# Values of a hybrid attention layer: projected with weights stationary and turned by transposing DMAs

## The chip, the cores and the metric

The kernel is one program on the 8 cores of a Trainium2 chip. Each core has a TensorE (PE, with its weight loads shown as PEld), a VectorE (DVE), a ScalarE (ACT), a GpSimd (POOL) and a SyncE (SP), and a share of 16 DMA engines. SP and POOL issue nearly all the DMAs. The metric is the device time of the slowest core in microseconds (us). Nothing passes between the cores.

## The reference

Two sequences of 4096 tokens with 2048 channels go through one layer. Cut to what matters:

```
h = rms_norm(x, norm_gain)
q, k, v, z_attn, u_pool, z_pool, gates = split(h @ w_in)     # q, k, v: 3 groups x 8 heads x 128
for g, (window, dilation) in enumerate(((128,1), (512,4), (2048,16))):
    qg, kg = partial_rope(rms_norm(q[g])), partial_rope(rms_norm(k[g]))
    o_g, lse_g = dilated_window_attention(qg, kg, v[g], window, dilation)
attn = softmax over the groups of lse, times o
y_attn = (attn * silu(z_attn)) @ w_branch_attn
y_pool = (multi-scale causal means of u_pool, mapped) * silu(z_pool) @ w_branch_pool
x = x + (sigmoid(gates) . (y_attn, y_pool)) @ w_out
```

Each of the three groups has 8 heads of 128 channels. A query of group g sees the keys t, t-d, t-2d, ... back to t-window.

## The kernel before

**Tiling.** A sequence is cut into four runs of own tokens for four cores; the second sequence does the same on cores 4 to 7. The table KINDS has three kinds of core: kind 0 (cores 0 and 4) has 1168 own tokens and no halo, kind 1 (cores 1 and 5) has 1008 and a halo of 1168, kind 2 (cores 2, 3, 6, 7) has 960 and a halo of 2048. The halo is what group 2, with its window of 2048, needs from before the core's own tokens. Tr and Hr are a sixteenth of the own tokens and of the halo. The program holds three arms and each core runs one; buffers of kind 1 have numbers near 150 to 200 in the profile, those of kind 2 near 240 to 290.

**Stages.** Stage 1 loads x in chunks (halo chunks 0 to 3 in buffers hTh, own chunks 5 and 6 in hX), norms them (squares on ACT, sums at line 756 on DVE for the first two chunks and on POOL for the rest, one matmul at line 760, scaling at line 791 on DVE), and projects keys and values of group 2 for halo and own tokens. They go to the DRAM tensors k2d and v2d. `late_copy` (line 813, on ACT) copies the last 512 halo tokens into hX, strided, since groups 0 and 1 need them. Stage 2 does the three attention groups head by head, stages 3 to 5 the pooling branch, the gates and the output projection.

**Keys and values.** A key projection has a 128 x 128 weight block as the stationary operand and up to 512 tokens moving, 16 matmuls deep (the 2048 channels). Its result has channels on the partitions. It is normed (lines 835 to 847; the sum of squares is a matmul at line 838) and rotated (`rope`, line 860: two small swap DMAs on SP, then three DVE operations). A value projection has it the other way round: tokens are stationary (up to 128 of them, taken with a stride of 1, 4, 8 or 16) and 512 weight columns, four heads, move. So the result has tokens on the partitions, as the product with the attention weights at line 1304 needs them. A tile with fewer than 128 tokens still takes 512 moving columns. Values of groups 0 and 1 are made for four heads at a time (`values`), in buffers vS0 and vS1.

**Order.** A planner (`Flow`) runs every process in an estimated time and writes each engine's instructions down in the order in which they became ready; on the chip each engine runs its list in order and waits on semaphores. It puts a DMA's data at a rate of 0.31 MB per us, and gives each operation a fixed estimate. Weights stream through POOL's queue (line 651, 1 MB of f32 each, cast to bf16) into 16 slots in stage 1 and 8 after it.

Of the kernel before, what the change touches and what calls it, by code (L numbers as in the profile page):

```python
# [400 lines left out]
def build_program():  # L401
    nc = bass.Bass("TRN2", target_bir_lowering=False)
    nwb = sum(4 if k == "v" else 1 for k, _ in weight_order())
# [51 lines left out]
def build_core(nc, sem, ps, io, kind_, Z):  # L455
# [59 lines left out]
    wsl, wq, B_w = [], [], []  # L515
    for hf in range(2):
        wt, _, _ = at(f"w{hf}", OW + 32768 * hf, [128, 8 * KC * 128], BF16)
        wsl += [wt[:, 2048 * i:2048 * i + 2048].rearrange("p (k n) -> p k n", n=128) for i in range(8)]
        wq += [wt[:, 8192 * i:8192 * i + 8192].rearrange("p (k n) -> p k n", n=512) for i in range(2)]
    for i in range(16):  # L520
        B_w.append(S.buf(f"w{i}", OW + 4096 * i, OW + 4096 * (i + 1)))
# [133 lines left out]
    def take(kind, n):  # L655
        k = wtake[0]
        size = 4 if kind == "v" else 1
        wtake[0] += size
        assert (W[k]["kind"], W[k]["n"]) == (kind, n), (W[k], kind, n)
        for j in range(size):  # L660
            yield ("wait", W[k + j]["ev"])
        return got(k, size)

    def got(k, size):
        pos = k if k < NFIRST else (k - NFIRST) % 8
        return dict(t=wq[pos // 4] if size == 4 else wsl[pos], slots=list(range(pos, pos + size)),
                    bufs=[B_w[pos + j] for j in range(size)], need=[W[k + j]["ev"] for j in range(size)])

    def take_later(kind, n):
# [102 lines left out]
    def scales():  # L772
        for c in PREP:
            n = Z.n[c]
            if c < 4:
# [982 lines left out]
```

How the kernel before makes its waits and increments, by code:

```python
        def run(ename, eng):  # L139
            w = {k: 0 for k in sems}
            for o in streams[ename]:
                for k, d in o.deps.items():
                    if d.eng == "pe" and ename == "pe" and not d.isdma:
                        continue
                    if w[k] < d.semval:
                        eng.wait_ge(sems[k], d.semval)
                        w[k] = d.semval
                ins = o.fn(eng)
                if o.signal:
                    ins.then_inc(sems[o.key], 16 if o.isdma else 1)
            for k, v in cnt.items():
                if w[k] < v:
                    eng.wait_ge(sems[k], v)
```

## Time and profile before

| | us |
|---|---|
| median of 3 runs | 1561.34 (1558.42 to 1572.68) |
| profiled execution, whole | 1558.15 |
| its span on the slowest core (core 1) | 1556.5 |
| spans of kind 0, cores 0 and 4 | 1534.1, 1534.8 |
| spans of kind 1, cores 1 and 5 | 1556.5, 1553.3 |
| spans of kind 2, cores 2, 3, 6, 7 | 1551.1, 1546.5, 1546.1, 1551.0 |
| PE busy on core 1 | 1463.6 (94%) |
| ACT, DVE, POOL busy on core 1 | 535.0, 600.0, 158.3 |

PE is named busy from the issue of a matmul to its modelled end, so its share says little on how densely it works. The distance between matmuls of a full stretch does: 512 matmuls of 512 or 496 columns take 108.8 us at the end of the program.

### The profile page before, as it was taken

The numbers are of one execution on the slowest core, as the hardware profiler recorded it, in microseconds if no ns is written. First come the engines' busy times: TensorE is split into PE (matmuls) and PEld (weight loads), VectorE is DVE, ScalarE is ACT, GpSimd is POOL, SyncE is SP. The second block draws the span as 40 slices with busy tenths as digits, with TensorE's granted clock in tenths as the row PEclk, the third lists the DMA queues.
The fourth block names the chain that finished last, engine by engine and source line by source line (L and its number), as shares of the span: only waits on it lengthen the run. The fifth ranks groups of instructions, "written<-read, shape, count | busy, mean of one in ns | idle before, by whom it ended". The sixth has DMA issues, their size and how long they took to land.

```text
span 1556.5 us, 22967 instructions; the slowest of 8 cores (1534.1 to 1556.5 us)
## 1 busy us (share of the span) xinstructions
PE 1463.6 (94%) x7644; PEld 784.6 (50%) x7644; DVE 600.0 (39%) x999; ACT 535.0 (34%) x924; POOL 158.3 (10%) x234
## 2 busy tenths in 40 slices
PE   2579779999999999999999999999999999999997
PEld 1344336659755545555645555544444444444443
DVE  3344166221001667663047767774211222222211
ACT  2554573332113656562155666421111111111000
POOL 1034340010000000000000000000000000000000
PEclk9789889999999999999999999999999999999998
DMA  7964241163524355443254453435444444444973
GB/s 144 172 170 108 83 127 51 44 118 73 112 55 85 68 104 96 70 99 63 43 104 95 75 98 61 85 69 97 78 72 80 78 72 82 80 82 68 226 196 102
DMA packets 98143, 147.19 MB, mean 95 GB/s; under 512 B 50464, under 2 KB 64416, under 8 KB 98016
## 3 DMA queue, kind: packets, MB, share of 16 engines
q0 software_dynamic: 23184, 84.42, 32.1%
q1 hardware_dynamic: 74208, 60.73, 14.0%
q8 instruction: 66, 1.08, 0.3%
q10 hardware_dynamic: 624, 0.46, 0.1%
q14 instruction: 61, 0.50, 0.1%
HBM read 206.95 MB, written 19.01 MB: 145 GB/s over the span
## 4 chain that ended last, share of the span: by engine, by line
PE 89%; DMA 3%; issue 3%; POOL 1%; DVE 1%; ACT 1%; SPq 1%; DVEq 0%; ACTq 0%; POOLq 0%
PE ps L821 68%; PE ps L1622 7%; PE ps L1572 7%; PE ps L838 2%; PE ps L1278 1%; PE ps L1304 1%; POOL s_acc L756 1%; PE ps L1308 1%; DMA s_rota_179<-s_kst_171 1%; PE ps L935 1%; DMA s_xs_159<-xc 1%; DMA s_rota_178<-s_kst_174 1%; DMA s_xs_158<-xc 1%; DMA s_rota_178<-s_kst_171 0%; PE ps L1478 0%
## 5 line engine op out<-in xcount | busy, mean ns | idle before, releaser
L821 PE MATMUL ps<-s_hX,s_w_156 128*128 128x512 bf16 (+3 forms) x3584 | 786.3, 372 | 0.0
L821 PEld LDWEIGHTS ps<-s_hX,s_w_156 128*128 128x128 bf16 x3584 | 351.0, 98 | 375.2 <-issue 4.9
L651 POOL DMA_DIRECT2D s_w_156<-wst x152 | 80.4, 530 | 1149.3 <-PE ps L821 824.5
L821 PE MATMUL ps<-s_w_156,s_hX 128*128 128x512 bf16 (+2 forms) x672 | 147.1, 379 | 0.0
L821 PEld LDWEIGHTS ps<-s_w_156,s_hX 128*128 128x128 bf16 (+2 forms) x672 | 82.5, 123 | 60.8
L1622 PE MATMUL ps<-s_mT,s_w_156 128*128 128x496 bf16 (+1 forms) x512 | 109.0, 376 | 0.0
L1622 PEld LDWEIGHTS ps<-s_mT,s_w_156 128*128 128x128 bf16 x512 | 50.1, 98 | 58.7
L847 DVE SCALAR_TENSOR_TENSOR s_kS_150<-ps,s_cst,s_rr_144 128x384 bf16<-128x384 f32 (+1 forms) x8 | 4.9, 609 | 187.6 <-PE ps L821 182.3
L842 ACT ACTIVATE s_rr_144<-ps 128x512 f32<-128x512 f32 (+3 forms) x72 | 38.0, 528 | 73.8 <-PE ps L838 66.6
L842 ACT ACTIVATE s_rr_145<-ps 128x512 f32<-128x512 f32 (+3 forms) x72 | 38.8, 539 | 61.1 <-PE ps L838 53.7
L1572 PE MATMUL ps<-s_pT,s_w_156 128*128 128x512 bf16 (+1 forms) x256 | 59.6, 376 | 0.0
L1572 PE MATMUL ps<-s_aT,s_w_156 128*128 128x512 bf16 (+1 forms) x256 | 59.6, 376 | 0.0
L821 PE MATMUL ps<-s_w_157,s_hX 128*126 128x512 bf16 x256 | 59.5, 394 | 0.0
L821 PEld LDWEIGHTS ps<-s_w_157,s_hX 128*126 128x126 bf16 x256 | 59.2, 323 | 0.3
L821 PE MATMUL ps<-s_w_157,s_hTh_147 128*73 128x512 bf16 x256 | 59.1, 388 | 0.0
L821 PE MATMUL ps<-s_w_157,s_hTh_148 128*73 128x512 bf16 x256 | 58.8, 391 | 0.0
L835 ACT ACTIVATE s_sq_142<-ps 128x512 bf16<-128x512 f32 (+3 forms) x72 | 38.1, 529 | 37.1 <-PE ps L821 36.0
L835 ACT ACTIVATE s_sq_143<-ps 128x512 bf16<-128x512 f32 (+3 forms) x72 | 38.5, 534 | 32.6 <-PE ps L821 30.0
L760 PE MATMUL ps<-s_acc,s_onesf 128*128 128x292 f32 (+2 forms) x12 | 8.2, 779 | 41.9 <-DVE s_acc L756 34.7
L821 PEld LDWEIGHTS ps<-s_w_157,s_hTh_148 128*73 128x73 bf16 x256 | 30.3, 118 | 27.4 <-issue 3.2
L821 PEld LDWEIGHTS ps<-s_w_157,s_hTh_147 128*73 128x73 bf16 x256 | 30.1, 117 | 27.2 <-issue 3.3
L838 PE MATMUL ps<-s_sq_142,s_ones 128*128 128x512 bf16 (+3 forms) x72 | 25.8, 359 | 18.9 <-ACT s_sq_142 L835 17.1
(308 smaller groups left out, 1532.8 us busy)
## 6 DMA issues: line engine op xcount, KB each, us to landing
s_w_156<-wst POOLq DMA_DIRECT2D x152, 512.0 KB, 5.3
s_w_157<-wst POOLq DMA_DIRECT2D x8, 512.0 KB, 10.3
v2d<-s_vst_175 SPq DMA_DIRECT2D x16, 128.0 KB, 2.1
v2d<-s_vst_176 SPq DMA_DIRECT2D x16, 128.0 KB, 2.0
v2d<-s_vst_177 SPq DMA_DIRECT2D x16, 128.0 KB, 2.1
s_v_199<-v2d SPq DMA_DIRECT2D x4, 512.0 KB, 4.3
s_v_189<-v2d SPq DMA_DIRECT2D x4, 512.0 KB, 4.5
s_xr_215<-xc SPq DMA_DIRECT2D x8, 256.0 KB, 4.0
```

The lines of the kernel that those rows point to most:

```text
L651: yield ("dma", "pool", 1048576, lambda g: g.dma_start(out=wsl[pos][:].rearrange("p k n -> p (k n)"), in_=wst[k]), after, [B_w[pos]], f"w{ ...
L756: yield ("op", eng, dur, lambda v, si=si, n=n: v.tensor_tensor(out=acc[:, 0:n], in0=acc[:, 0:n], in1=sqf[si][:, 0:n], op=ALU.add), [B_acc, ...
L821: yield ("op", "pe", mm_us(n), lambda t, kc=kc, a=lhs(kc), b=rhs(kc): t.matmul(ps[i][0:nr, 0:n], lhsT=a, rhs=b, start=(kc == 0), stop=(kc ...
L835: yield ("op", "act", act_us(n), lambda a: a.activation(out=sq[si][:, 0:n], in_=ps[i][:, 0:n], func=AF.Square), [B_ps[i]], [B_sq[si]])
L838: yield ("op", "pe", mm_us(n), lambda t: t.matmul(ps[ax][:, 0:n], lhsT=ones[:], rhs=sq[si][:, 0:n], start=True, stop=True), [B_sq[si], B_o ...
L842: yield ("op", "act", act_us(n), lambda a: a.activation(out=rr[ri][:, 0:n], in_=ps[ax][:, 0:n], func=AF.Ln, bias=float(128 * EPS)), [B_ps[ ...
L935: yield ("op", "pe", mm_us(n), lambda t, kc=kc, b=mov(kc): t.matmul(ps[i][:, 0:n], lhsT=w["t"][:, kc, :], rhs=b, start=(kc == 0), stop=(kc ...
L1278: yield ("op", "pe", mm_us(n), lambda t, kap=kap, qap=qap, e0=e0, n=n: t.matmul(ps[si][0:rows, e0:e0 + n], lhsT=kap, rhs=qap, start=True, ...
L1304: yield ("op", "pe", mm_us(n), lambda t, vap=vap, nr=nr, e1=e1, cc=cc, n=n, go=go, end=end: t.matmul(nu[:, cc:cc + n], lhsT=vap, rhs=Eb[ei ...
L1308: yield ("op", "pe", mm_us(nd), lambda t, dap=dap, k=k: t.matmul(de[:, c0:c0 + nd], lhsT=ones[0:rows], rhs=dap, start=(k == 0), stop=(k == ...
L1572: b=src[:, h, t0:t0 + n]: t.matmul(ps[yi][:, 0:n], lhsT=a, rhs=b, start=(h == 0), stop=(h == 7)), w["bufs"] + [B_src[h]], [B_ps[yi]])
L1622: b=mT[:, db, t0:t0 + n]: t.matmul(ps[i][:, 0:n], lhsT=a, rhs=b, start=(db == 0), stop=(db == KC - 1)), w["bufs"] + [B_mT[db]], [B_ps[i]])
```

## The change

Values are projected as keys are: a 128 x 128 weight block of one head is stationary and the tokens move. The result has channels on the partitions, and has to be turned. In stage 1 each piece goes to v2d as it is, and the load of a head's v2 tile is a transposing DMA. In stage 2 values of groups 0 and 1 are evacuated by ACT into buffers vt0 and vt1, and a transposing DMA on SP (`turned`) writes the token tiles vS0 and vS1, which are now for one head and double-buffered. The weights of the values come one block for each head. The tokens are split 1184/1024/944/944. The halo of kind 1 has three chunks (444, 370, 370 columns) instead of four of 292. The halo copy is cut into 8 pieces for each chunk and runs on POOL at a lower priority. The load of the masks and the tables and two memsets wait for the last values of stage 1.

```
-KINDS = ((1168, 0), (1008, 1168), (960, 2048))
+KINDS = ((1184, 0), (1024, 1184), (944, 2048))
...
-    o = [("b", BK + 16 + h) for h in range(8)] + [("v", 48 + 16), ("v", 48 + 20)]
+    o = [("b", BK + 16 + h) for h in range(8)] + [("b", BV + 16 + h) for h in range(8)]
+    for h in range(8):
+        o += [("b", BV + h), ("b", BV + 8 + h), ("b", BK + h), ("b", BQ + h), ("b", BK + 8 + h), ("b", BQ + 8 + h),
+              ("b", BQ + 16 + h), ("b", BZA + h)]
...
+        k = -(-16 // (512 // self.Hr)) if H else 0
+        self.halo = list(range(k))
+        cut = [-(-16 * c // k) for c in range(k + 1)] if H else []
+        self.res = {c: (cut[c], cut[c + 1] - cut[c]) for c in self.halo}
...
-        yield ("op", "act", 2.0, lambda a: a.copy(out=dst, in_=src), B_hTh[hi], [B_late[c]])
+        r0, k = Z.res[c]
+        for kc in range(0, KC, 2):
+            yield ("op", "pool", 1.2, lambda g, kc=kc: g.tensor_copy(out=dst[:, kc:kc + 2], in_=src[:, kc:kc + 2]),
+                   B_hTh[hi][kc:kc + 2], [B_late[c]])
...
+    def spill(h, c, src, B, t, sem_, done):
+        k = 128 * (Z.to if c == "own" else Z.res[c][1])
+        yield ("dma", "sp", 131e3, lambda s: s.dma_start(
+            out=v2d[h, :, 128 * t:128 * t + k], in_=src[:, 0:k]), [B], [B_v2d[(h, c)]], sem_)
...
+    def value_piece(c, h, i):
+        yield ("op", "act", act_us(n), lambda a: a.copy(
+            out=vst[vi][:, 0:128 * k].rearrange("p (r l) -> p r l", r=k)[:, :, 0:Hr],
+            in_=ps[i][:, 0:n].rearrange("p (r l) -> p r l", r=k)), [B_ps[i]], [B_vst[vi]])
...
+    def own_piece(vi, m, i, cnt, e):
+        yield ("op", "act", act_us(n), lambda s: s.copy(
+            out=vst[vi][:, 0:128 * k].rearrange("p (r l) -> p r l", r=k)[:, :, l0:l0 + n // k],
+            in_=ps[i][:, 0:n].rearrange("p (l r) -> p r l", r=k)), [B_ps[i]], [B_vst[vi]])
...
+        if H:
+            first += [(c, "v", h) for h in range(NHEAD) for c in (C0, C1)]
...
+        seq = [(5, "k")] + [(c, what) for c in Z.halo[2:] for what in "kv"] + [(6, "k")] if H else []
...
+        for h in range(NHEAD):
+            w = w2[("v", h)]
+            for m, (a, n) in enumerate(own):
+                i = yield from project(P_pp, lambda kc: w["t"][:, kc, :], lambda kc: hX[:, kc, a:a + n], n,
+                                       lambda kc: rd(kc) + w["bufs"])
+                F.spawn(own_piece(vi, m, i, cnt, e), HIGH)
...
-            part(lambda s: s.dma_start(out=v2[i][:, 0:16, :], in_=v2d[h, :, 0:16, :]), hv, B_v2[i], f"lv{i}")
-        part(lambda s: s.dma_start(out=v2[i][:, t0:NV2, :], in_=v2d[h, :, t0:NV2, :]), ov, B_vo[i], f"lw{i}")
+        part(lambda s: s.dma_start_transpose(out=v2[i][:], in_=v2d[h, :, 0:128 * NV2]),
+             [B_v2d[(h, c)] for c in Z.halo + ["own"]], [B_v2[i], B_vo[i]], f"lv{i}")
...
+    def values(g, h, V):
+        w = yield from take("b", BV + 8 * g + h)
+        a0 = LT - (128, 512)[g] * hp
+        for a, n in pieces(a0, NX):
+            i = yield from project(P_pp, lambda kc: w["t"][:, kc, :], lambda kc: hX[:, kc, a:a + n], n,
+                                   lambda kc: rd(kc) + w["bufs"])
+            F.spawn(v_evac(i, dst, n, B_vt, cnt, e), HIGH)
+        F.spawn(turned(g, V, e), MID)
+
+    def turned(g, V, e):
+        vi = yield ("acq", P_vS[g])
+        yield ("wait", e)
+        yield ("dma", "sp", 300e3, lambda s: s.dma_start_transpose(out=vs[vi][:], in_=vt[:]), [B_vt], [B_v[vi]],
+               f"tv{g}{vi}")
...
+        for h in range(NHEAD):
+            V = [{}, {}, None]
+            for g in range(2):
+                yield from values(g, h, V[g])
+            for g in range(3):
+                if g < 2:
+                    yield from keys(g, h, K)
+                yield from queries(g, h, Q)
+                F.spawn(unit(g, h, K, Q, V[g]), MID)
+            yield from gate_z(h)
```

**SP, one head in stage 2, kind 1.** Before, a head's rows on SP are the loads of the keys and values of group 2 for a later head, and the swaps of `rope` (rotb is their target):

```order
L860 DMA s_rotb_204<-s_kS_151 16x1136 x2
L1045 DMA s_k_198<-k2d 128x16x73
L1048 DMA s_k_198<-k2d 128x1008
L1050 DMA s_v_199<-v2d 128x2048
L1055 DMA s_v_199<-v2d 128x1024
L860 DMA s_rotb_203<-s_qT_155 16x1008 x2
L860 DMA s_rotb_204<-s_kS_153 16x1520 x2
```

In the changed kernel a head's rows on SP are these, from its first value tile to its last query:

```order
L1108 DMA_TRANSPOSE s_vS_231<-s_vt_228 128x9x128
L1059 DMA s_k_234<-k2d 128x16x74
L1062 DMA s_k_234<-k2d 128x1024
L1065 DMA_TRANSPOSE s_v_235<-v2d 128x24x128
L1108 DMA_TRANSPOSE s_vS_233<-s_vt_229 128x12x128
L859 DMA s_rotb_240<-s_kS_169 16x1152 x2
L859 DMA s_rotb_239<-s_qT_173 16x1024 x2
L859 DMA s_rotb_240<-s_kS_171 16x1536 x2
L859 DMA s_rotb_239<-s_qS_237 16x1024 x2
L859 DMA s_rotb_240<-s_qS_238 16x1024 x2
```

Three transposing DMAs, of 9, 24 and 12 tiles of 128 x 128, now stand in one row ahead of all five swaps of the head.

**PE, start of stage 2, kind 1.** Before, the values of four heads come first, tokens stationary (a row's first number is how many):

```order
L821 MATMUL ps<-s_w_156,s_hX 128x512 x128
L821 MATMUL ps<-s_w_156,s_hX 112x512 x16
L821 MATMUL ps<-s_w_156,s_hX 128x512 x32
L821 MATMUL ps<-s_w_156,s_hX 124x512 x16
L821 MATMUL ps<-s_w_156,s_hX 128x512 x32
```

In the changed kernel one head's values of groups 0 and 1 come first (weights 174 and 175), then its keys and queries (176, 177):

```order
L820 MATMUL ps<-s_hX,s_w_174 128x384 x48
L820 MATMUL ps<-s_hX,s_w_175 128x512 x48
L820 MATMUL ps<-s_hX,s_w_176 128x384 x24
L837 MATMUL ps<-s_sq_160,s_ones 128x384
L820 MATMUL ps<-s_hX,s_w_176 128x384 x16
L837 MATMUL ps<-s_sq_161,s_ones 128x384
L820 MATMUL ps<-s_hX,s_w_176 128x384 x8
L820 MATMUL ps<-s_hX,s_w_177 128x512 x6
```

What stood once ahead of four heads, 18 + 24 tiles of 16 matmuls for two quads, now stands in each head's own rows, 6 pieces of 16 matmuls.

**POOL, stage 1, kind 1, changed kernel.** The sums of squares (line 752, acc) of chunk 5 and the pieces of the copy of chunk 1 (line 811):

```order
L752 TENSOR_TENSOR s_acc<-s_acc,s_sqf_200 128x512
L654 DMA s_w_189<-wst 128x2048
L811 COPY s_hX<-s_hTh_166 128x2x5x32 x2
L752 TENSOR_TENSOR s_acc<-s_acc,s_sqf_198 128x512
L811 COPY s_hX<-s_hTh_166 128x2x5x32
L752 TENSOR_TENSOR s_acc<-s_acc,s_sqf_199 128x512
L811 COPY s_hX<-s_hTh_166 128x2x5x32
L752 TENSOR_TENSOR s_acc<-s_acc,s_sqf_200 128x512
```

Before, nothing but sums stood here; the copy was one instruction on ACT.

## Rows read from the trace of the kernel before

**Rows 1.** The cores: span and granted TensorE clock.

```profile
core 0: 1534.1 us, clock 0.984
core 1: 1556.5 us, clock 0.977
core 2: 1551.1 us, clock 0.983
```

**Rows 2.** Windows, core 1: stretch, length, busy us (instructions) by engine, clock, DMA, GB/s.

```profile
30.00:107.00 77.00, 48.31 (x267) 30.86 (x268) 33.33 (x82) 40.32 (x62) 13.01 (x17) 0.80 0.84 184
178.00:230.00 52.00, 35.39 (x142) 15.14 (x141) 24.62 (x37) 35.98 (x49) 21.88 (x22) 0.84 0.33 100
230.00:408.00 178.00, 178.00 (x925) 128.41 (x924) 52.10 (x123) 55.33 (x112) 11.84 (x17) 1.00 0.31 68
408.00:1057.00 649.00, 648.27 (x3751) 352.33 (x3750) 340.60 (x515) 309.64 (x542) 41.27 (x75) 1.00 0.44 82
```

**Rows 3.** Chain of waits, core 1, last stretch: start us, us, what.

```profile
1436.75 108.81 PE ps L1622 x512
```

**Rows 4.** Timeline, PE of core 1, tail of stage 1: start us, us, instructions.

```profile
320.51 4.97 PE L821 MATMUL ps<-s_hX,s_w_156 128*128 128x496 bf16 x23
...
353.11 55.01 PE L821 MATMUL ps<-s_w_157,s_hX 128*126 128x512 bf16 x238
```

**Rows 5.** Groups of ACT, core 1, by form: busy us, mean ns, idle before.

```profile
L813 ACT COPY s_hX<-s_hTh_147 128x2048 bf16<-128x2048 bf16 x2 | 17.7, 8856 | 7.2 <-DVE s_hTh_147 L791 7.2
L1061 ACT CAST s_vS_197<-ps 128x512 bf16<-128x512 f32 x16 | 9.4, 586 | 45.9 <-PE ps L821 45.9
```

**Rows 6.** Timeline, core 1, one copy and the four matmuls after copies.

```profile
45.97 0.40 PE L838 MATMUL ps<-s_sq_142,s_ones 128*128 128x292 bf16 x1 [5.05 <-ACT s_sq_142 L835]
...
101.05 0.40 PE L838 MATMUL ps<-s_sq_142,s_ones 128*128 128x292 bf16 x1 [5.71 <-ACT s_sq_142 L835]
...
172.92 8.89 ACT L813 COPY s_hX<-s_hTh_147 128x2048 bf16<-128x2048 bf16 x1
...
190.18 0.59 PE L838 MATMUL ps<-s_sq_142,s_ones 128*128 128x512 bf16 x1 [6.37 <-ACT s_sq_142 L835]
...
225.95 0.58 PE L838 MATMUL ps<-s_sq_143,s_ones 128*128 128x512 bf16 x1 [10.24 <-ACT s_sq_143 L835]
```

**Rows 7.** Timeline, PE of core 2: matmuls after copies, own value tiles.

```profile
58.12 0.58 PE L838 MATMUL ps<-s_sq_235,s_ones 128*128 128x512 bf16 x1 [3.61 <-ACT s_sq_235 L835]
...
209.68 0.56 PE L838 MATMUL ps<-s_sq_235,s_ones 128*128 128x480 bf16 x1 [6.07 <-ACT s_sq_235 L835]
...
394.52 25.69 PE L821 MATMUL ps<-s_w_250,s_hX 128*120 128x512 bf16 x116
```

**Rows 8.** DMA issues, core 1: queue, count, KB each, median us to landing.

```profile
s_v_199<-v2d SPq DMA_DIRECT2D x4, 512.0 KB, 4.3
...
s_k_198<-k2d SPq DMA_DIRECT2D x4, 292.0 KB, 6.0
s_rotb_204<-s_qS_202 SPq DMA_DIRECT2D x8, 31.5 KB, 1.9
s_w_156<-wst POOLq DMA_DIRECT2D x152, 512.0 KB, 5.3
```

**Rows 9.** Timeline, core 1, first head: query swap, first scores.

```profile
500.35 1.12 SPq L860 DMA_DIRECT2D s_rotb_204<-s_qS_201  x2
...
509.14 0.61 PE L1278 MATMUL ps<-s_qS_201,s_kS_150 128*128 128x128 bf16 x6
```

**Rows 10.** Groups of POOL, core 1, by form.

```profile
L756 POOL TENSOR_TENSOR s_acc<-s_acc,s_sqf_166 128x512 f32<-128x512 f32 x5 | 7.2, 1442 | 15.2 <-ACT s_sqf_166 L732 14.7 <-POOL s_acc L756 0.4
L696 POOL MEMSET s_vst_175<- 128x512 bf16 x1 | 0.5, 524 | 6.2 <-issue 6.2
```

**Rows 11.** Timeline, core 1: POOL's sums end a wait; last scaling.

```profile
159.08 1.31 PE L760 MATMUL ps<-s_acc,s_onesf 128*128 128x292 f32 x2 [4.34 <-POOL s_acc L756]
...
259.06 0.72 DVE L791 SCALAR_TENSOR_TENSOR s_hX<-s_xs_165,s_gsc,s_rsb 128x496 bf16<-128x496 f32 x1
```

More of the change, by code:

```diff
@@ L495, in build_core @@
     hX, _, o = at("hX", o, [128, KC, NX], BF16)
-    B_late = [S.buf(f"late{c}") for c in range(4)]
+    B_late = [S.buf(f"late{c}") for c in Z.halo]
     B_own = [[S.buf(f"own{m}_{kc}") for kc in range(KC)] for m in range(len(own))]
@@ L514, in build_core @@
     OW = (max(o, o_h) + 63) // 64 * 64
[L515 to L521, printed above, removed]
+    wsl, B_w, _ = many("w", 16, OW, [128, KC, 128], BF16)
     X = OW + 8 * 4096
@@ L617, in build_core @@
     LOW, MID, HIGH = 8, 4, 1
-    W = []
-    for k, (kind, n) in enumerate(WO):
-        W += [dict(ev=Ev(), kind=kind, n=n, part=j) for j in range(4 if kind == "v" else 1)]
+    W = [dict(ev=Ev(), kind=kind, n=n) for kind, n in WO]
     E_x = {}
-    PREP = [0, 1, 5, 2, 3, 6] if H else [5, 6, 7]
+    PREP = ([0, 1, 5] + Z.halo[2:] + [6]) if H else [5, 6, 7]
     C0, C1 = PREP[:2]
@@ L655, in take, with take_later @@
     def take(kind, n):
[L656 to L669, printed above, removed]
+        w = take_later(kind, n)
+        yield ("wait", w["need"])
+        return w
+    def take_later(kind, n, uses=1):
         k = wtake[0]
         wtake[0] += 1
-        assert (W[k]["kind"], W[k]["n"]) == (kind, n) and kind == "b"
-        return got(k, 1)
+        assert (W[k]["kind"], W[k]["n"]) == (kind, n), (W[k], kind, n)
+        pos = k if k < NFIRST else (k - NFIRST) % 8
+        return dict(t=wsl[pos], pos=pos, bufs=[B_w[pos]], need=W[k]["ev"], uses=uses)
     def drop(w):
-        for i in w["slots"]:
-            F.release(P_w[i], i)
+        w["uses"] -= 1
+        if w["uses"] == 0:
+            F.release(P_w[w["pos"]], w["pos"])
     def consts():
@@ L798, in scales @@
             if c < 4:
-                F.spawn(late_copy(c), MID)
-    E_late = [Ev() for _ in range(4)]
-    halo_uses = {c: [3] for c in range(4)}
+                F.spawn(late_copy(c), LOW)
+    E_late = [Ev() for _ in Z.halo]
+    halo_uses = {c: [2 * NHEAD + 1] for c in Z.halo}
     def halo_done(c):
@@ L878, in build_core @@
     B_k2d = {(h, c): S.buf(f"k2d{h}_{c}") for h in range(NHEAD) for c in PREP}
-    B_v2d = {(qd, t): S.buf(f"v2d{qd}_{t}") for qd in range(2) for t in range(NV2)}
+    B_v2d = {(h, c): S.buf(f"v2d{h}_{c}") for h in range(NHEAD) for c in Z.halo + ["own"]}
     k2col = {c: Z.off[c] for c in PREP}
@@ L929, in lane @@
         mov, rd = chunk_at(c)
-        for j in w["need"]:
-            yield ("wait", j)
+        yield ("wait", w["need"])
         n = Z.n[c]
@@ L955, in stage1 @@
             i = yield ("acq", P_pp)
-            F.spawn(lane(c, h, i, kw[h]), 6 + 0.01 * k)
-        for h in range(8):
-            for e in kw[h]["need"]:
-                yield ("wait", e)
-        if H:
-            seq = [(0, "v"), (1, "v"), (5, "k"), (2, "k"), (2, "v"), (3, "k"), (3, "v"), (6, "k"), (6, "v")]
-        else:
-            seq = [(7, "v")]
+            F.spawn(lane(c, what, h, i, w2[(what, h)]), 6 + 0.01 * k)
+        for k in range(NHEAD):
+            yield ("wait", w2[("v", h)]["need"])
@@ L1002, in load_tabb @@
     def load_tabb():
+        for h in range(NHEAD):
+            yield ("wait", E_v2d[(h, "own")])
         yield ("dma", "sp", 150e3, lambda s: s.dma_start(out=msk[:], in_=msk_d), [], [B_msk], "c1")
@@ L1015, in pads @@
                     yield ("op", "pool", 0.3, lambda g, t=t, n=n, w=w: g.memset(t[:, n:w], 0.0), [], [b])
+        F.fire(E_pad)
+        for h in range(NHEAD):
+            yield ("wait", E_v2d[(h, "own")])
         if H:
@@ L1027, in load_kv2 @@
                 yield ("wait", E_k2d[(h, c)])
-            for t in range(NV2):
-                yield ("wait", E_v2d[(h // 4, t)])
+            for c in Z.halo + ["own"]:
+                yield ("wait", E_v2d[(h, c)])
             F.spawn(load_k2(h, i), MID)
```

246 lines of the change are left out of this document (109 added, 137 removed).

## The prediction, made before the changed kernel ran

> **What bounds the kernel now.** I read the cores first [rows 1]: core 1, of kind 1, sets the span of 1556.5 us, core 2 stands 5.4 us behind, core 0 22.4 us. Then the windows of core 1 [rows 2]: from 230 us on PE is busy for the whole of each stretch at a granted clock of 1.00, with DMA at 0.31 and 0.44; before 230 us it is busy 48.31 of 77 us and 35.39 of 52, at 0.80 and 0.84. So there are two problems. Behind 230 us only fewer or cheaper matmul columns shorten the time, and ACT, DVE and the DMAs matter only if they become late. Ahead of it the norm of x and its helpers matter.
>
> The price of a column comes from the last stretch of the chain [rows 3]: 512 matmuls, half of 512 and half of 496 columns, in 108.81 us, which is 108.81/(512 x 504) = 0.4217 ns, or 215.9 ns for 512 columns.
>
> **Columns.** A value tile costs 512 columns for each of its 16 matmuls however few tokens it holds, while the new form pays for the tokens alone. I counted matmuls times columns in the two programs. On kind 1 the halo values were 16 tiles x 2 quads x 16 matmuls x 512 = 262,144 columns; they become 8 heads x 16 x 1184 = 151,552, or 110,592 fewer. Its other values come out equal (1008 tokens already filled the tiles: 131,072, 147,456 and 196,608 either way), and 16 more own and 16 more halo tokens add 40,192 elsewhere. Net 70,400 fewer, x 0.4217 ns = **-29.7 us**. On kind 2 the halo of 2048 filled its tiles already; the three sets of own values lose 10,240 columns each and 16 fewer tokens 37,952: 68,672, or **-29.0 us**. Kind 0 loses 130,368, or **-55.0 us**.
>
> Own values in stage 1 were also dearer than their columns. The 126-token stationaries of core 1 took 55.01/238 = 231.1 ns each [rows 4] against 215.9; 256 of them give **-3.9 us** when contiguous weights take their place.
>
> **The halo copy.** On ACT one copy of 2048 elements in each partition takes 8856 ns, 4.3 ns for an element [rows 5]. Key pieces behind it wait: the first sum-of-squares matmul after each of the four copies stood 5.05, 5.71, 6.37 and 10.24 us behind ACT, 27.4 us in all [rows 6]; on core 2 the same four run from 3.61 to 6.07 us [rows 7]. Not all of this comes back, since ACT has the squares of the next chunk to do in that place too and PE starts earlier into the next wait. I take two thirds, **-18 us** on core 1, -13 on core 2. The stretch from 178 to 230 us ran at clock 0.84 [rows 2], 52 x 0.16 = 8.3 us lost; with shorter gaps I take half back, **-4 us**, and claim nothing for core 2, for which I give no such row.
>
> **The start.** Kind 1's first halo chunk has 444 columns instead of 292, the second 370 instead of 292. With 2048 channels of four bytes that is 1.25 and 0.64 MB more before the keys of these chunks can run. At the 184 GB/s of the stretch from 30 to 107 us [rows 2] they take 6.8 and 3.5 us: **+10 us**. Later chunks are smaller to the same total and lie behind the projections.
>
> **The transposing DMAs** are in no row of before. In stage 2 a head issues three on SP, of 9, 24 and 12 tiles of 128 x 128, ahead of all its rope swaps. The lower bound for a tile is that of a plain load of the same bytes: 512 KB of v2, 16 tiles, land in 4.3 us, 0.27 us for one. The upper bound is one small DMA after another, each with the 1.9 us that a 31.5 KB swap takes to land [rows 8]. What is covered? Between the first transposing DMA of a head and the first swap that its queries need, PE has its group 1 values (48 x 512 columns, 10.4 us), its group 0 keys (48 x 384, 7.8) and its first query piece (32 x 512, 6.9): 25.1 us, with attention matmuls left out. Less the 6.0 us of the k2 loads among them and the 1.9 us of a swap, some 17.2 us remain for 45 tiles, if SP's queue finishes each before the next: **0.38 us for a tile is the threshold**. The query swap has no slack of its own: it was issued at 500.35, and the first scores ran at 509.14 when the rotated query was ready [rows 9]. I take 0.3 us, near the lower bound, since a transposing DMA of 768 KB moves the bytes of a load and not those of a swap. That is below the threshold, so I count nothing here. The middle of the two bounds, 1.08 us, would decide otherwise (rival A).
>
> DMA: Bandwidth & Descriptors, section "Latency and other measured facts", of the Trainium skill gives transposing DMAs 261 GB/s effective; an estimate from it is 0.13 us for a tile of 32 KB, and the sum stays as it is. No run here shows it yet.
>
> **The copy on POOL.** It is 8 pieces of 256 to 384 elements for each chunk, among the sums of squares (1442 ns each at 512 columns). A bf16 memset of 512 elements takes 524 ns on POOL [rows 10], which bounds a piece from below at 0.33 us; ACT's 4.3 ns for an element bounds it from above at 1.66 us; so 2.6 to 13 us for a chunk. PE waits for POOL's sums already (4.34 us in one place [rows 11]). I take the lower half and nothing in the sum, since it runs at low priority; the upper half is rival C.
>
> **At nothing, with cover.** Weights: 8 loads for a head, 5.3 us each [rows 8], under 7 to 10 us of PE for a block; without that cover it would be 5 us for a block. Evacuations on ACT: a cast takes 586 ns [rows 5], a strided one at worst 4.3 ns x 512 = 2.2 us, under the 3.46 us that PE spends on a piece. The tail of stage 1: PE reaches the last own key chunk at 320.51 [rows 4], while its scaling ended at 259.06 [rows 11]; 47 us less work ahead of it leaves some 14 us. The table load waits for the last spill, but its data is wanted over 25 us later. Memsets run on a POOL that is idle there.
>
> **Sum.** Core 1: 1556.5 - 29.7 - 3.9 - 18 - 4 + 10 = 1511. Core 2: its 120-token stationaries ran at 25.69/116 = 221.5 ns [rows 7], 256 x 5.6 ns = 1.4 us too dear; 1551.1 - 29.0 - 1.4 - 13 = 1508. Core 0: 1534.1 - 55.0 = 1479. Core 1 stays the slowest. The profiled execution took 1558.15, 1.65 us above its span, so 1512.5; the median shown, 1561.34, is 3.2 above the profiled one. **Forecast 1515 us.** Its own range is 1488 (all of the ACT waits and of the clock come back, 14 more, and the first chunk costs nothing, 10 more, with 3 for the spread) to 1530 (only a sixth of the waits and no clock comes back).
>
> **Rivals.**
> - *A, slower: the transposing DMAs hold SP's queue.* Swaps, and behind them rope and scores, come late once a tile takes over 0.38 us; each 0.1 us more is 45 x 0.1 x 8 heads = 36 us. At 0.5 us the time is 1515 + 43 = 1558, at the middle of the bounds, 1.08, it is 1515 + 252 = **1767**, at 1.9 it is 2062. For it: three large DMAs ahead of each head's swaps in one queue, and a query swap without slack [rows 9]. Against: plain DMAs of that size run 0.27 us for 32 KB [rows 8], and planned order keeps some attention work between. Chance 0.20. The Trainium skill, VectorE: DVE Perf Modes, section "The three transpose paths", has a figure on this side: 1309 ns for one 128 x 128 transpose by DMA. If it holds for tiles in a row, an estimate is 1515 + (1.309 - 0.38) x 45 x 8 = 1849. Tiles that cost more than the 1.08 us of the middle have 0.06 of A's 0.20. This figure of the Trainium skill and the one above lie on both sides of the threshold, and no run here decides yet.
> - *C: the front stays bound, now by POOL.* The pieces push the sums of squares back, PE waits as long as it did for ACT, and the 22 us are not recovered: **1537**, up to 1546 if the pieces cost 13 us for a chunk. For it: POOL's waits already show [rows 11], and the larger first chunks delay every later one. Against: POOL is busy only 21.88 of 52 us in the stretch before 230 us [rows 2]. Chance 0.16.
> - *The forecast*, no new wait in stage 2 and part of the front back: 0.64.
>
> The likeliest case gives 1515. The range goes from 1487 to 1565: forecast and C hold 0.80, with the mild end of A. Within 1% of 1561.34 (about what a measurement of this kernel can tell) lies between 1546 and 1577: A from 0.47 to 0.55 us and the far end of C, 0.07. Faster: 0.64 + 0.14 = 0.78. Slower: 0.15.
>
> **What would show it.** Right: spans near 1511, 1508 and 1479 on cores 1, 2 and 0; stage 2 of core 1 beginning well before 408 us; no sum-of-squares matmul waiting 5 us for ACT in the front; transposing DMAs of 24 tiles landing in 7 us or less; value matmuls at 0.42 ns for a column. Wrong: 24 tiles landing in over 9 us with PE waiting for rope's DVE steps in every head (A); POOL copies over 1 us with PE waiting on s_acc before 230 us (C); halo or own value matmuls dearer than keys, or a span of core 2 above core 1, since I left its front almost untouched.

## The result, and the profile after

The changed kernel took 1523.06 us (median of 4 runs, 1509.58 to 1536.31), the kernel before 1560.21 us beside it. The ratio is **0.9667, with an interval of 0.9580 to 0.9754**: 2.5 to 4.2% faster. Two of the four runs (1533.95 and 1536.31 us) count as slow and are left out of it; the medians of all runs give 0.976, and the control below, which does the same work, 0.979. The profiled execution took 1509.58 us, where the forecast was 1515 for the median and 1512.5 for a profiled one.

The cores [rows 1]: span and granted clock, six of the eight.

```profile
core 0: 1484.0 us, clock 0.982
core 1: 1485.0 us, clock 0.990
core 2: 1504.0 us, clock 0.987
core 3: 1507.9 us, clock 0.986
core 4: 1503.3 us, clock 0.978
...
core 7: 1507.3 us, clock 0.986
```

Core 1 fell by 71.5 us and no longer sets the end; cores 3 and 7 of kind 2 do. Cores 0 and 4 run the same work and stand 19 us apart.

The windows of core 1, those of [rows 2]:

```profile
30.00:107.00 77.00, 57.88 (x268) 28.87 (x269) 43.02 (x82) 29.12 (x60) 31.33 (x27) 0.89 0.95 210
178.00:230.00 52.00, 49.88 (x286) 27.41 (x284) 46.06 (x65) 26.49 (x53) 31.41 (x21) 1.00 0.23 75
230.00:408.00 178.00, 177.71 (x941) 88.58 (x940) 55.61 (x102) 65.69 (x118) 16.65 (x21) 1.00 0.52 102
408.00:1057.00 649.00, 649.00 (x3847) 348.28 (x3845) 338.60 (x499) 289.47 (x507) 39.58 (x75) 1.00 0.53 87
```

PE gains in the front: 57.88 us busy instead of 48.31 in the first window and 49.88 instead of 35.39 in the second, at clocks of 0.89 and 1.00 instead of 0.80 and 0.84. From 230 us on it was full and is full (177.71 of 178 us, then 649.00 of 649). The price of a column is the old one: the last stretch of the chain [rows 3] has 512 matmuls of 512 columns now, 110.52/(512 x 512) = 0.4216 ns.

```profile
1363.54 110.52 PE ps L1642 x512
```

The waits of PE on core 1 in the first 300 us (total us, times, longest). Before, two of them were:

```profile
PE ps L760 <- DVE s_acc L756: 34.7, 2, 27.2
PE ps L760 <- POOL s_acc L756: 7.2, 2, 4.3
```

After:

```profile
PE ps L756 <- DVE s_acc L752: 30.8, 1, 30.8
PE ps L837 <- ACT s_sq L834: 9.3, 2, 9.0
PE ps L956 <- DVE s_hTh L787: 7.7, 3, 3.0
PE ps L756 <- POOL s_acc L752: 6.7, 2, 5.7
```

The waits for ACT's squares were four in [rows 6], 27.4 us; 9.3 are left, 9.0 of them in one place. The copy that was behind them is now on POOL (min, median and longest ns of one):

```profile
L811 POOL COPY s_hX<-s_hTh x24: 1543/1712/3531, 41.7 to 211.3; 128x320 bf16<-128x320 bf16 x16, 128x384 bf16<-128x384 bf16 x8
```

The transposing DMAs of core 1 (count, median us from issue to landing), and SP's list from a head's first one to its key swap:

```profile
s_vS<-s_vt SPq DMA_TRANSPOSE x16, 7.5
s_v<-v2d SPq DMA_TRANSPOSE x8, 7.4
```

```profile
477.04 1.32 SPq L1108 DMA_TRANSPOSE s_vS<-s_vt  x1
478.52 0.51 SPq L1059 DMA_DIRECT2D s_k<-k2d  x1
479.13 4.58 SPq L1062 DMA_DIRECT2D s_k<-k2d  x1
483.86 5.30 SPq L1065 DMA_TRANSPOSE s_v<-v2d  x1
489.79 1.27 SPq L1108 DMA_TRANSPOSE s_vS<-s_vt  x1
500.74 1.15 SPq L859 DMA_DIRECT2D s_rotb<-s_kS  x2
```

24 tiles land in 7.4 us, 0.31 us for a tile; the 9 and the 12 tiles of the value buffers take as long, 7.5 us. From the first issue to the last landing some 20.3 us pass (489.79 + 7.5 - 477.04). Issuing the three takes SP 1.32 + 5.30 + 1.27 = 7.9 us, and it is free again 9.7 us before the key swap is issued. So no query waits in a usual head. The first head of core 4 is different (SP's list, then PE's):

```profile
216.43 28.64 SPq L1108 DMA_TRANSPOSE s_vS<-s_vt  x2
245.18 1.19 SPq L859 DMA_DIRECT2D s_rotb<-s_kS  x2
```

```profile
263.84 2.72 PE L820 MATMUL ps<-s_hX,s_w 128*128 128x384 bf16 x8 [19.66 <-DVE s_qS L846]
```

There the two DMAs took 29.1 and 32.4 us to land, weight loads beside them 20 to 29 us, and the swap behind them 14.8. PE stood for 19.66 us. On core 3 the same place cost 1.0 us, and on cores 0 and 7 nothing.

### The profile page after: what moved, and what is told of

It reads as the page before. It is cut to its first block, busy times and chain, and to the rows that moved or that the text cites. A ratio compares the mean times of both kernels' runs of the same rounds, so it can differ in the third digit from the quotient of the medians.

```text
span 1507.9 us, 23338 instructions; the slowest of 8 cores (1484.0 to 1507.9 us)
## 1 busy us (share of the span) xinstructions
PE 1427.8 (95%) x7740; PEld 725.8 (48%) x7740; DVE 638.3 (42%) x999; ACT 514.2 (34%) x926; POOL 234.6 (16%) x268
## 3 DMA queue, kind: packets, MB, share of 16 engines
q0 software_dynamic: 23184, 84.42, 34.8%
q1 hardware_dynamic: 83808, 75.45, 18.3%
## 4 chain that ended last, share of the span: by engine, by line
PE 86%; DMA 4%; POOL 3%; DVE 2%; issue 2%; SPq 1%; ACT 1%; ACTq 0%; DVEq 0%; POOLq 0%
PE ps L820 63%; PE ps L1642 7%; PE ps L1592 7%; PE ps L956 3%; POOL s_acc L752 3%; DMA s_rota<-s_kst 2%; DMA s_xs<-xc 2%; PE ps L1299 2%; PE ps L837 2%; PE ps L1325 2%; PE ps L1329 1%; DVE s_rota L870 1%; PE ps L756 0%; SPq L714 0%; DVE s_hTh L787 0%
## 5 line engine op out<-in xcount | busy, mean ns | idle before, releaser
L820 PE MATMUL ps<-s_hX,s_w 128*128 128x480 bf16 (+4 forms) x4608 | 931.3, 356 | 1.0 <-DVE s_qS L846 1.0
L820 PEld LDWEIGHTS ps<-s_hX,s_w 128*128 128x128 bf16 x4608 | 450.4, 98 | 418.1 <-issue 2.0
L654 POOL DMA_DIRECT2D s_w<-wst x160 | 84.7, 529 | 1115.7 <-PE ps L820 859.2
L956 PE MATMUL ps<-s_hTh,s_w 128*128 128x512 bf16 x512 | 122.6, 400 | 5.4 <-DVE s_hTh L787 4.2
L841 ACT ACTIVATE s_rr<-ps 128x512 f32<-128x512 f32 (+4 forms) x144 | 80.0, 556 | 130.1 <-PE ps L837 120.6
L820 PE MATMUL ps<-s_hTh,s_w 128*128 128x512 bf16 x512 | 113.9, 379 | 0.0
L834 ACT ACTIVATE s_sq<-ps 128x512 bf16<-128x512 f32 (+4 forms) x144 | 79.6, 554 | 76.4 <-PE ps L820 56.9
L1642 PE MATMUL ps<-s_mT,s_w 128*128 128x464 bf16 (+1 forms) x512 | 102.1, 362 | 0.0
L752 POOL TENSOR_TENSOR s_acc<-s_acc,s_sqf 128x512 f32<-128x512 f32 (+2 forms) x60 | 92.8, 1546 | 54.5 <-ACT s_sqf L728 44.5
L844 ACT ACTIVATE s_rr<-s_rr 128x512 f32<-128x512 f32 (+4 forms) x144 | 84.9, 590 | 11.6
L956 PEld LDWEIGHTS ps<-s_hTh,s_w 128*128 128x128 bf16 x512 | 52.1, 102 | 75.7 <-issue 22.0
L820 PEld LDWEIGHTS ps<-s_hTh,s_w 128*128 128x128 bf16 x512 | 50.0, 98 | 60.4 <-issue 0.5
L1642 PEld LDWEIGHTS ps<-s_mT,s_w 128*128 128x128 bf16 x512 | 50.1, 98 | 51.9
```

The source lines that it names most:

```text
L654: yield ("dma", "pool", 1048576, lambda g: g.dma_start(out=wsl[pos][:].rearrange("p k n -> p (k n)"), in_=wst[k]), after, [B_w[pos]], f"w{ ...
L752: yield ("op", eng, dur, lambda v, si=si, n=n: v.tensor_tensor(out=acc[:, 0:n], in0=acc[:, 0:n], in1=sqf[si][:, 0:n], op=ALU.add), [B_acc, ...
L820: yield ("op", "pe", mm_us(n), lambda t, kc=kc, a=lhs(kc), b=rhs(kc): t.matmul(ps[i][0:nr, 0:n], lhsT=a, rhs=b, start=(kc == 0), stop=(kc ...
L834: yield ("op", "act", act_us(n), lambda a: a.activation(out=sq[si][:, 0:n], in_=ps[i][:, 0:n], func=AF.Square), [B_ps[i]], [B_sq[si]])
L841: yield ("op", "act", act_us(n), lambda a: a.activation(out=rr[ri][:, 0:n], in_=ps[ax][:, 0:n], func=AF.Ln, bias=float(128 * EPS)), [B_ps[ ...
L844: yield ("op", "act", act_us(n), lambda a: a.activation(out=rr[ri][:, 0:n], in_=rr[ri][:, 0:n], func=AF.Exp, scale=-0.5), [B_rr[ri]], [B_r ...
```

## The experiments

All kernels of the study find their arm by comparing the kind in turn, not by a jump table. The first run is the control for that. The spans given are those of the profiled executions. For the copy on ACT and the DMAs one at a time there is no ratio on record, so those two are read from their spans alone.

**Control.** In place of the switch, for each engine:

```
-            for k in eng.Switch(eng.snap(reg), n=len(KINDS)):
-                runs[k](name, eng)
+            for k in range(len(KINDS)):
+                with eng.If_eq(reg, k):
+                    runs[k](name, eng)
```

> The changed kernel with one difference, which all the kernels of this study have: each engine finds its arm by comparing the kind with 0, 1 and 2 in turn, instead of by a jump table. Every theory expects the spans of the changed kernel within 5 us (cores 1, 2 and 3 near 1485, 1504 and 1508) and a time near 1510. Where it differs, the other runs are compared with this one.

Measured: ratio to the kernel before 0.9789 (0.9724 to 0.9853), profiled 1523.47 us; cores 0, 1 and 2 at 1484.4, 1483.7 and 1509.9, but core 3 at 1520.3 and core 7 at 1521.9, 12 and 15 us above the changed kernel. The median, 1522.56 us, is that of the changed kernel. Part of the rise is again the first head: PE waits there 8.6 us on core 3, 6.6 on core 7 and 1.6 on core 2, for DVE s_qS. The cores of kind 2 vary by 10 us and more between runs of the same work, so below only larger differences count on them. Two waits of core 1, for comparison:

```profile
PE ps L757 <- DVE s_acc L753: 31.8, 2, 30.7
PE ps L838 <- ACT s_sq L835: 8.5, 3, 8.0
```

**The halo copy back on ACT.**

```
-        for kc in range(0, KC, 2):
-            yield ("op", "pool", 1.2, lambda g, kc=kc: g.tensor_copy(out=dst[:, kc:kc + 2], in_=src[:, kc:kc + 2]),
-                   B_hTh[hi][kc:kc + 2], [B_late[c]])
+        yield ("op", "act", 2.0, lambda a: a.copy(out=dst, in_=src), B_hTh[hi], [B_late[c]])
...
-                F.spawn(late_copy(c), LOW)
+                F.spawn(late_copy(c), MID)
```

> The changed kernel with the halo copy back on ACT, one instruction for each chunk at the old priority; all else as changed. Main theory (the copies on ACT made PE wait for the squares, and these waits with the lower clock around them were some 18 us and more on core 1, 13 us on cores 2 and 3): PE waits for ACT s_sq before 240 us go from about 10 us on core 1 back to 25 or more; the spans of cores 2, 3, 6, 7 grow from about 1505 by 10 to 20 us, that of core 1 from 1485 by 18 to 40 us; the time is near 1523 against 1510. Rival (the waits are those of the next chunk's squares, and the copy only filled the same place): all spans within 4 us of the changed kernel's.

Measured, PE's waits on core 1:

```profile
PE ps L757 <- DVE s_acc L753: 38.8, 2, 31.7
PE ps L836 <- ACT s_sq L833: 25.2, 3, 10.6
```

The waits for ACT are back at 25.2 us, the profiled time is 1534.88 us, and the span of core 1 grows by 25.5 us against the control (1509.2), of core 5 by 23.2; cores 2, 3, 6 and 7 grow by 18.3, 13.0, 15.6 and 7.8. The main theory holds. The copy on POOL is worth some 25 us on kind 1 and 8 to 18 us on kind 2. Without PE's waits for s_qS in the first head (1.6, 8.6, 0 and 6.6 us on cores 2, 3, 6 and 7 of the control; 0, 0.4, 0.8 and 0.5 here) the four cores of kind 2 grow by 19.9, 21.2, 14.8 and 13.9. The copy on POOL was not measured in the kernel before, without the other changes.

**Kind 1's halo in four chunks.**

```
-        k = -(-16 // (512 // self.Hr)) if H else 0
+        k = 4 if H else 0
```

> The changed kernel with kind 1's halo in four chunks of 296 columns instead of 444, 370 and 370; cores 2, 3, 6, 7 and 0, 4 run the same work. Theory of the prediction (a larger first chunk costs 10 us at the start, since its x arrives later): PE's first projection on core 1 starts some 4 us or more earlier, and the span of core 1 falls from 1485 to about 1475. Rival (three larger chunks gave core 1 more than they cost: fewer norms, fewer waits, longer stretches of PE, higher clock in the front): core 1 gets slower by 8 to 20 us, to 1493 to 1505, and its clock falls from 0.990. In both cases the time stays at that of cores 2, 3, 6, 7, near 1510.

Measured: core 1 at 1503.7 (20.0 more than the control) with clock 0.983, core 5 at 1500.4 (16.2 more). Core 1 took 1498.3 to 1513.9 us in all four executions, and 1482.9 to 1484.6 in those of the control. The waits of core 1:

```profile
PE ps L757 <- DVE s_acc L753: 36.7, 2, 25.0
PE ps L957 <- DVE s_hTh L788: 10.9, 3, 8.3
...
PE ps L821 <- DVE s_kst L847: 4.2, 1, 4.2
PE ps L838 <- ACT s_rr L842: 3.6, 3, 2.5
PE ps L957 <- DVE s_kst L847: 2.7, 1, 2.7
```

The smaller first chunk does start PE earlier, after 25.0 us instead of 30.7. But the second chunk's sums now cost 11.7 us where they cost 1.1 in the control, pieces wait in more places, for DVE above all, and the clock is lower. The rival holds: larger chunks, which the prediction charged with 10 us, bring 16 to 20. The time does not show it (ratio to before 0.9783, 0.9732 to 0.9835), since kind 2 ends last.

**Each value transposing DMA of stage 2 twice.**

```
-        yield ("dma", "sp", 300e3, lambda s: s.dma_start_transpose(out=vs[vi][:], in_=vt[:]), [B_vt], [B_v[vi]],
-               f"tv{g}{vi}")
+        for _ in range(2):
+            yield ("dma", "sp", 300e3, lambda s: s.dma_start_transpose(out=vs[vi][:], in_=vt[:]), [B_vt], [B_v[vi]],
+                   f"tv{g}{vi}")
```

> The changed kernel with each transposing DMA of the stage 2 values issued twice into the same buffer; the second waits on SP until the first has landed, so SP is held some 7.5 us longer at each of two places of a head, some 15 to 22 us for a head in all. The trace of the changed kernel has the last transposing DMA of a head issued about 11 us before the head's first swap. Main theory (SP has this slack and about 8 us more before a swap delays PE): with the held time around the slack, 0 to 5 us for a head on cores 1, 2, 3, so the time is between unchanged and 40 us more. Rival (the queue's hold is what decides and there is no slack, the threshold of 17 us for a head as worked out): 15 to 22 us for each of 8 heads less the 3 left, so 95 to 150 us more. Second rival (these DMAs are so well covered that nothing is seen at all): within 4 us.

Measured: ratio to before 1.0668 (1.0623 to 1.0713), 1669.71 us. Core 1 is only 20 us slower than the control (1504.0), core 3 is 151 us slower (1671.2). On core 3 the v2 loads, which are not doubled, land late, and PE waits for the queries:

```profile
s_vS<-s_vt SPq DMA_TRANSPOSE x32, 6.6
s_v<-v2d SPq DMA_TRANSPOSE x8, 26.1
```

```profile
PE ps L821 <- DVE s_qT L847: 105.5, 4, 30.2
PE ps L821 <- DVE s_qS L847: 39.2, 3, 29.8
```

These two waits are 144.7 of the 151 us. The size is the first rival's (95 to 150 us), the reason is not: a constant hold of the queue would cost core 1 and core 3 about alike, since SP is free 6.6 to 9.7 us before the key swap in a usual head of core 1 in the changed kernel, and 7.4 to 8.9 us on core 3. What differs is the landing, 26.1 us on core 3 and 10.2 on core 1, against 6.8 and 7.4 in the changed kernel. In one such stretch the clock goes with it (windows of core 3):

```profile
600.00:640.00 40.00, 33.93 (x212) 18.47 (x209) 11.42 (x16) 15.16 (x28) 2.11 (x4) 0.97 1.13 94
640.00:663.00 23.00, 0.00 (x0) 0.00 (x0) 1.75 (x3) 0.00 (x0) 0.00 (x0) 0.50 0.85 61
663.00:700.00 37.00, 36.47 (x208) 19.63 (x209) 22.05 (x39) 19.69 (x37) 2.11 (x4) 0.92 0.36 65
```

From 600 to 663 us the packets' times add up to 1.13 and 0.85 of the span of the core's 16 DMA engines, and these move only 94 and 61 GB/s; PE stands for 23 us, its granted clock falls to 0.50 (1.2 GHz) and is 0.92 on average in the stretch after.

**One at a time.** Over these five profiles (the changed kernel's too), all 48 transposing DMAs that took more than 16 us to land had another one in flight. That alone is weak, since of all 1088 only 269 were alone from issue to landing, and a DMA that lands late meets the next one by that. So I tried a wait for the one before (a buffer that each of them writes):

```
+    B_one = S.buf("one")
...
-        yield ("dma", "sp", 300e3, lambda s: s.dma_start_transpose(out=vs[vi][:], in_=vt[:]), [B_vt], [B_v[vi]],
+        yield ("dma", "sp", 300e3, lambda s: s.dma_start_transpose(out=vs[vi][:], in_=vt[:]), [B_vt], [B_v[vi], B_one],
...
-             [B_v2d[(h, c)] for c in Z.halo + ["own"]], [B_v2[i], B_vo[i]], f"lv{i}")
+             [B_v2d[(h, c)] for c in Z.halo + ["own"]], [B_v2[i], B_vo[i], B_one], f"lv{i}")
```

> The control with one added wait: each transposing DMA waits on SP until the one before it has landed, so never two are in flight. In the runs so far every transposing DMA that took over 16 us to land (48 of them, 20 to 40 us, with weight loads beside it late as well) had a second one in flight with it, and none of 391 that were alone. New theory (two in flight together can slow all DMAs of the core): no landing over 16 us in any core, no PE wait of 5 us or more for DVE s_qS or s_qT; the added hold of SP is 1 to 3 us for a head and lies in its slack; cores 2, 3, 6 and 7 at 1500 to 1510, cores 0 and 4 near 1484, the time 1505 to 1515 against the control's 1517 to 1523. Rival (these slow landings come from the weights or from other cores, and the pair is chance): slow landings come as often, and the times stay at the control's. Second rival (the added wait costs more than it saves): 8 heads x 3 us or more slower than the control.

Measured: profiled 1526.20 us; cores 1, 2 and 3 at 1494.6, 1520.6 and 1524.6. One landing in 192 is still over 16 us, two in the control. PE now waits in the first head on every core of kinds 1 and 2, 4.0 to 12.3 us. One less among 192 shows nothing. Core 1, which had no slow landing in the control, is 10.9 us slower, and the new wait in its first head is 6.5 of them. So the added wait costs something and saves nothing that can be seen; of the second rival the sign holds on cores 1, 2 and 3, not the size. This version was meant to beat both kernels and did not.

**The same wait in the kernel with each one twice.**

> The kernel that issued each transposing DMA of stage 2 values twice (1670 us), with the same added wait: never two in flight. SP is held longer than in that kernel, by what is left of the v2 landing, some 2 to 6 us for a head. New theory (two in flight slow all DMAs): the loss of 147 us against the control mostly goes, cores 2 and 3 come to 1510 to 1560 (SP's slack of 11 us for a head is now overdrawn by up to 5 us), no landing over 16 us. Rival (the hold of SP is what costs): still slower, 1680 us or more.

Measured: ratio to before 1.0301 (1.0270 to 1.0333), 1612.13 us. Of 320 landings in the profiled execution (1644.22 us) 16 are over 16 us, each with no other transposing DMA in flight, against 44 in that of the kernel without the wait (1672.77 us). The added wait takes away some 58 us of the median, but two in flight are not the whole cause: the theory that they are needed has fallen. In the two kernels with the wait all 17 slow landings are v2 loads, which read DRAM (17 of 128); none of the 384 from the buffers vt0 and vt1 is slow. What makes a landing slow stays open. Slow landings overlap weight loads in every case, but a landing of 20 us or more can hardly miss them, as a block is loaded every 7 to 10 us. Keeping weight loads apart from transposing DMAs was not tried, and whether the traffic of the other cores plays a part was not tested.

**The form of the values alone** (old split, four chunks, copy on ACT; the edits are those above and below).

> The form of the values alone: values projected like keys and turned by transposing DMAs, but with the token split of before (1168, 1008, 960, 960), kind 1's halo in four chunks, and the halo copy on ACT in one instruction. Theory of the prediction (columns become time at 0.4217 ns each): kind 0 loses 174,080 columns, 73 us, to about 1461; kind 1 loses 110,592, 46.6 us, and 3.9 of dear stationaries, to about 1506; kind 2 loses 24,576 in partly filled tiles, 10.4 us and 1.4, to about 1539; the time is near 1543, ratio 0.988. Rival (the saved columns lie under other waits or are paid back by the new steps in stage 2): cores 1 and 5 gain less than half of the 50 us. Second rival: stage 2 collects slow landings and the time is above 1550.

Measured against the profiled execution before: core 0 -65.5 us and core 4 -64.6 (expected -73), core 1 -48.4 and core 5 -51.9 (expected -50), core 2 -0.2, core 3 +17.1, cores 6 and 7 +23.7 and +26.1 (expected -12). The ratio is 1.0127 (1.0100 to 1.0154): this part alone makes the kernel *slower*, by 1.0 to 1.5%. On kind 2 PE waits 9.6, 17.3, 18.3 and 23.8 us (cores 2, 3, 6 and 7) for DVE s_qS in the first head; without these waits the four cores stand at -9.8, -0.2, +5.4 and +2.3. Cores 6 and 7 ran at granted clocks of 0.962 and 0.961 besides, where cores 2 and 3 had 0.980 and 0.976, so that their rise is not all due to that wait.

**The old token split alone.**

```
-KINDS = ((1184, 0), (1024, 1184), (944, 2048))
+KINDS = ((1168, 0), (1008, 1168), (960, 2048))
...
```

> The changed kernel with the token split of before alone. Theory (a token costs its columns): kind 2 gets 16 more tokens with 44,096 columns, 18.6 us more, so cores 2, 3, 6, 7 come to 1523 to 1535 and the time to about 1530 to 1540; kind 1 loses 16 own and 16 halo tokens, 40,192 + 6,144 + 4,096 columns at most, 17 to 21 us, to about 1465; kind 0 loses some 18 us, to about 1466. Rival (part of the tokens' cost lies in waits of the front): cores 2 and 3 move by 8 us or less.

Measured: ratio to before 0.9994 (0.9963 to 1.0025). Against the control, cores 0 and 1 fall by 15.9 and 17.4 us, as expected; cores 2, 3, 6 and 7 rise by 33.8, 26.8, 19.7 and 31.2, more than the 18.6 expected. The first head of core 7 shows the rest (SP's list, PE's wait, and the windows):

```profile
431.08 13.67 SPq L1066 DMA_TRANSPOSE s_v<-v2d  x1
...
454.21 26.92 SPq L1066 DMA_TRANSPOSE s_v<-v2d  x1
481.28 4.48 SPq L1109 DMA_TRANSPOSE s_vS<-s_vt  x2
485.87 1.61 SPq L860 DMA_DIRECT2D s_rotb<-s_kS  x2
```

```profile
491.33 2.96 PE L821 MATMUL ps<-s_hX,s_w 128*128 128x480 bf16 x7 [26.73 <-DVE s_qS L847]
```

```profile
440.00:460.00 20.00, 20.00 (x112) 10.85 (x111) 2.50 (x4) 8.29 (x17) 1.59 (x3) 1.00 1.31 72
460.00:480.00 20.00, 4.61 (x23) 1.96 (x20) 0.00 (x0) 2.96 (x5) 0.00 (x0) 0.75 1.30 115
```

Two v2 loads, of head 0 and head 1, stand ahead of the first key swap. They took 40.0 and 31.1 us to land here, 12.6 and 14.0 on core 3 of the changed kernel. Without these waits (20.1, 20.4, 7.3 and 26.7 us; in the control 1.6, 8.6, 0 and 6.6) the four cores rise by 15.3, 15.0, 12.4 and 11.1: somewhat less than the 18.6 of the columns. Why the landings of the first head are slower with 960 tokens than with 944 was not tested.

## Why the prediction was right, and where it was not

The time was right by way of kind 2, which was put at 1508 and came to 1504.0 and 1507.9 on cores 2 and 3. The forecast itself was worked out from core 1, which was put at 1511, as the slowest, and came to 1485.0. The statement that core 1 stays the slowest is wrong. That 1515 held, although the sum behind it was 26 us too high, is luck: the sum of kind 2 stood only 3 us below it.

- **Core 1, term by term.** The form of the values gave -48.4 us and the split +17.4, together -31.0 (the sum had -33.6); the copy gave -25.5 (the sum had -22, with the clock), the chunks -20.0 (the sum had +10). That is -76.5 in all, and the control stands 72.8 us below the kernel before.
- **Kind 2, term by term.** Without the waits for s_qS in the first head, core 2 has -9.8 for the form, -15.3 for the split and -19.9 for the copy, -45.0 in all, and core 3 -0.2, -15.0 and -21.2, -36.4 in all; the control, counted in the same way, stands 42.8 and 34.8 us below the kernel before. The sum had -30.4 for form and split and -13 for the copy. So the columns brought less than was worked out and the copy more, and that the total of -43.4 fits is in part luck. On cores 6 and 7 the terms add up to 13 us too little; there the run of the form alone had the lower clock.
- **Columns: right.** The form alone gave core 1 -48.4 us where 46.6 + 3.9 were worked out, and the split moved core 1 by 17.4 where its 40,192 columns alone make 16.9. Kind 0 got 90% of its columns' price in the run of the form alone (65.5 of 73 us). On kind 2 the form brought less than its 12 us.
- **The halo copy: right in kind and size of the waits, the clock too small.** The ACT waits of core 1 fell by 18 us (27.4 to 9.3), the -18 of the sum. On kind 2 the copy was worth 14 to 21 us where 13 were taken. The clock was charged with -4. The mean granted clock of core 1 rose from 0.977 to 0.990, which is 35.8 - 14.9 = 21 us of full clock; where PE stands anyway this costs nothing, so the terms overlap.
- **The start: wrong in sign.** "+10 us" counted the x that a larger chunk must wait for. The first wait did rise, from 27.2 to 30.8 us, 3.6 instead of 6.8. But the second chunk's wait of 7.5 us (34.7 - 27.2) is gone, presumably since PE has more work on a chunk while the next comes in, and the front runs at a higher clock. With four chunks core 1 was 20 us slower. From +10 to -16 or -20 is 26 to 30 us, and that is where the 26 us between 1511 and 1485 come from.
- **The transposing DMAs: no wait in a usual head, as forecast, but 0.3 us a tile holds for one of the three only, and the first head was not looked at.** 24 tiles took 0.31 us each, as was taken. But 9 and 12 tiles took 7.5 us as well, so the time does not go by the tile, and the three together take 7.5 + 7.4 + 7.5 = 22.4 us, 0.50 us for each of 45 tiles. That is over the threshold of 0.38, and at 0.5 us rival A had put 1558. No wait came of it, because the k2 loads, for which 6.0 us had been set aside, ran beside the transposing DMAs: from the first issue to the last landing 20.3 us passed, of 17.2 + 6.0 = 23.2. So the outcome was right in part by luck. SP is held by the issue alone, 7.9 us. The first head has the v2 loads of two heads ahead of its first swap, and SP issues the swap at once behind them, so a landing that comes late there is paid by PE. Rival A happens at this one place: 0 to 1 us on most cores of the profiled execution, 8.0 on core 5, 19.7 on core 4, and up to 26.7 with the old split. The count of tiles does not explain the size, since cores 1 and 5 do the same work and PE waits 0.3 and 8.0 us. What differs is the landing (the latest of the value buffers' DMAs took 8.7 us on core 1, 15.4 on core 5), and what makes one late is open. A did not come in eight heads, as it was priced.
- The Trainium skill, VectorE: DVE Perf Modes, section "The three transpose paths", has 1309 ns for one 128 x 128 transpose by DMA; here 24 tiles in one DMA took 0.31 us each in the median, and the measurement decides. The Trainium skill, DMA: Bandwidth & Descriptors, section "Latency and other measured facts", led to an estimate of 0.13 us; no landing of 24 tiles here was that short, the shortest took 5.1 us, 0.21 us for a tile.
- **The copy on POOL: dearer than its upper bound, and still hidden.** 1308 ns for 256 elements on core 3 and 1712 ns in the median on core 1, some 14 us for a chunk against at most 13. Rival C did not follow: PE's waits for POOL's sums are 6.7 us, before 7.2.
- **The signs.** Two of the signs of being right did not come: one sum-of-squares matmul still waited 9.0 us for ACT, and 24 tiles took 7.4 us instead of 7 or less. Two of the signs of being wrong came: core 2 ended above core 1, and POOL copies took over 1 us with PE waiting on s_acc. The last one cannot tell C apart, since PE waited on s_acc before as well.

## What to carry over

What a part is worth depends on which core ends last: the form of the values freed kinds 0 and 1 by 48 to 66 us and alone made the kernel slower, and it took the token split to hand the freed time on. For a queue, look at its fullest place, here the first pass of the loop, where loads for two passes come together and no slack is left for a landing that comes late. A larger first chunk delays the start by its bytes, but may end the wait for the second one: work out both.

## What the runs showed of the hardware that was not expected

- In the nine profiles of kernels that have them, transposing DMAs of 24 tiles land in 5 to 16 us in 381 of 432 cases, and in 16 to 45 us in 51; the DMAs beside them are slow too, weight loads of 512 KB with up to 38 us instead of 5.3. In the windows shown the DMA engines are busy and move 61 to 115 GB/s. Of 320 transposing DMAs 44 were slow where two could be in flight and 16 where only one could, so two are not needed. DMAs of 9 to 12 tiles take as long as those of 24 (7.5 and 7.4 us).
- POOL copies bf16 at about 5 ns for an element of a partition (1308 ns for 256), slower than ACT's 4.3 in [rows 5], though its memset takes 1 ns (524 ns for 512, [rows 10]).
